# Attention of a hybrid block in half-height matmuls on eight cores: scores in three paired steps, values in two banks, filler in pairs of outputs

## The reference, cut to what matters

```python
q_nope, q_pe = q[..., :128], q[..., 128:]          # 128 + 64 dimensions
k_nope, v = kv[..., :128], kv[..., 128:]           # kv from the 512-wide latent c_kv
q_pe = apply_rope(q_pe, cos, sin); k_pe = apply_rope(k_rope, cos, sin)   # k_pe shared by all heads
sc = (q_nope . k_nope + q_pe . k_pe) * 192 ** -0.5   # key chunk <= query chunk, chunks of 64
out = softmax(sc) @ v;  y_attn = out * silu(z_attn)
```

## Time and profile before

| | |
|---|---|
| runs shown | 2835.36, 2835.76 (median), 3141.82 us |
| profiled execution | 2835.46 us |
| its span, slowest core (core 2) | 2832.8 us; all cores 2824.6 to 2832.8 us |
| granted TensorE clock, mean of cores | 0.994 to 0.997 of full speed |
| attention | from 1669 to 2376 us of the span |
| one head (heads 1 to 6, each) | 45.12 to 45.13 us |

### The profile page before, as it was taken

The page is one execution under the profiler, slowest core; times in us unless marked ns, Lnnn a source line. Parts: engine busy times, 40 slices in busy tenths (PEclk is TensorE's granted clock), DMA queues, the critical chain, the costliest instruction groups (busy, mean ns, idle before and its releaser), DMA issues.

```text
span 2832.8 us, 44730 instructions; the slowest of 8 cores (2824.6 to 2832.8 us)
## 1 busy us (share of the span) xinstructions
PE 2753.8 (97%) x16732; PEld 1563.5 (55%) x16732; DVE 985.0 (35%) x1675; ACT 819.0 (29%) x1365; POOL 376.5 (13%) x705
## 2 busy tenths in 40 slices
PE   6999999999999999999899999999999999999997
PEld 2455555555555554444799965555555554444443
DVE  3221112112211211111355546666666674121114
ACT  4210000000000001111476645656566563110013
POOL 0000000000000000000000014333333434000000
PEclk9999999999999999999999999999999999999998
DMA  9745555554545445554666420010100009954448
GB/s 262 142 74 79 83 79 81 80 83 79 80 79 82 79 80 81 94 99 77 186 191 205 147 42 16 16 23 16 24 16 16 16 1 198 232 87 78 80 83 283
DMA packets 94579, 265.66 MB, mean 94 GB/s; under 512 B 23968, under 2 KB 26144, under 8 KB 93344
## 3 DMA queue, kind: packets, MB, share of 16 engines
q0 software_dynamic: 39376, 148.91, 33.1%
q1 hardware_dynamic: 54992, 113.90, 13.2%
HBM read 390.71 MB, written 20.97 MB: 145 GB/s over the span
## 4 chain that ended last, share of the span: by engine, by line
PE 92%; DMA 3%; ACT 2%; issue 1%; POOL 1%; SPq 1%; DVE 1%; DVEq 0%; ACTq 0%; POOLq 0%
PE psall L290 92%; ACT arena L294 1%; DMA arena<-xo 1%; POOL arena L858 1%; DMA arena<-xres 1%; SPq L396 1%; DMA arena<-xt 1%; DVE arena L301 0%; DMA arena<-w_out_t 0%; SPq L392 0%; POOL arena L909 0%; DVEq L232 0%; ACT arena L297 0%; DVE arena L304 0%; ACTq L167 0%
## 5 line engine op out<-in xcount | busy, mean ns | idle before, releaser
L290 PE MATMUL psall<-arena 128*128 128x512 bf16 (+5 forms) x16732 | 2753.8, 327 | 59.1 <-ACT arena L294 22.6
L290 PEld LDWEIGHTS psall<-arena 128*128 128x128 bf16 x16732 | 1563.5, 98 | 1248.8 <-issue 96.7
L301 DVE TENSOR_TENSOR arena<-psall,arena 128x512 f32<-128x512 f32 (+3 forms) x378 | 225.6, 598 | 1252.9 <-PE psall L290 1230.2
L294 ACT ACTIVATE arena<-psall 128x512 bf16<-128x512 f32 (+7 forms) x706 | 447.5, 676 | 641.5 <-PE psall L290 426.3
L294 ACT ACTIVATE arena<-arena 128x768 bf16<-128x768 f32 (+7 forms) x487 | 313.0, 679 | 894.4 <-DVE arena L301 804.8
L301 DVE TENSOR_TENSOR arena<-arena 128x1024 f32<-128x1024 bf16 (+11 forms) x565 | 470.6, 847 | 194.4 <-ACT arena L294 117.5
L858 POOL TENSOR_SCALAR arena<-arena 128x64 bf16<-128x64 bf16 x512 | 258.4, 509 | 431.4 <-ACT arena L294 386.8
L363 POOL DMA_DIRECT2D arena<-w_in_t x95 | 67.1, 707 | 1292.5 <-PE psall L290 1195.7
L304 DVE TENSOR_SCALAR arena<-arena 128x192 bf16<-128x192 f32 (+3 forms) x440 | 137.7, 372 | 60.7 <-DMA arena<-xo 39.9
L297 ACT ACTIVATE arena<-arena 128x512 bf16<-128x512 f32 x64 | 40.3, 630 | 377.3 <-DVE arena L301 371.7
L307 DVE SCALAR_TENSOR_TENSOR arena<-arena 128x192 bf16<-128x192 f32 (+2 forms) x112 | 83.4, 750 | 76.0 <-ACT arena L294 69.3
(11 more groups left out here) (10 smaller groups left out, 9.4 us busy)
## 6 DMA issues: line engine op xcount, KB each, us to landing
arena<-w_in_t POOLq DMA_DIRECT2D x95, 1024.0 KB, 10.5
arena<-xt SPq DMA_DIRECT2D x128, 384.0 KB, 4.8
arena<-w_out_t POOLq DMA_DIRECT2D x64, 512.0 KB, 5.3
arena<-xo SPq DMA_DIRECT2D x32, 528.0 KB, 11.3
arena<-xres SPq DMA_DIRECT2D x6, 2048.0 KB, 47.3
out<-arena SPq DMA_DIRECT2D x8, 1536.0 KB, 12.5
arena<-w_uq_t POOLq DMA_DIRECT2D x16, 512.0 KB, 5.2
yc_spill<-arena SPq DMA_DIRECT2D x16, 256.0 KB, 8.1
```

The costliest lines, as they stand in the source:

```text
L290: P.add("pe", lambda e: e.matmul(out_, lhsT, rhs, start=start, stop=stop), reads=reads, writes=writes)
L294: P.add("act", lambda e: e.activation(out=out_, in_=in_, func=func, scale=scale, bias=bias), reads=reads, writes=writes)
L301: P.add(eng, lambda e: e.tensor_tensor(out=out_, in0=a, in1=b, op=op), reads=reads, writes=writes)
```

## The change

It touches attention and the first lines of the output projection.

1. Every matmul of attention uses 64 rows (partitions 0 to 63 or 64 to 127 of both operands; `LOHI`), issued in pairs, one of each row half, into two different banks. `mmr` records which row half last wrote a bank; when the other half writes it next, TensorE gets a wait on its own earlier matmul.
2. The rotary queries are folded: `q_out` writes the products to `TP`, a matmul with `dmat_bf` (ones at equal index modulo 64) sums the two parts, and `r_out` stores the result twice in `TQ`. Scores are then three pairs per unit instead of four matmuls: step 0 (tile 0 with rows 0 to 63, tile 1 with rows 64 to 127), step 1 (crosswise), step 2 (the rotary part, 64 rows for each tile).
3. Values: each key tile is two half matmuls, the lower rows into bank 4, the upper into bank 5, for either half of the queries. At the end of a half ScalarE copies bank 4 to `POS` and VectorE adds bank 5. `PV` of a half's first unit is held until the next unit.
4. The filler makes two outputs at a time, in banks 6 and 7, in two phases (each output gets one row half per phase), in chunks of four 512-column pairs. 26 chunks per head: 8 queries, 8 keys, 2 rotary sums, 8 values. A unit takes one chunk after `PV` and sometimes a second after `QK`; a chunk that starts a pair is only taken at the first place, where the sums of a half (`fin_b`) go too.
5. `fin_b` has four half matmuls in banks 6 and 7, a ScalarE copy, a VectorE addition, then Ln and Exp. There are two `ACC` instead of three.
6. The order of units is half 0 and then half 1, in each the widest and the narrowest in alternation (g = 0, 7, 1, 6, ... and 0, 15, 1, 14, ...). Within a unit `QK` step 0 comes first, then `PV` and filler, then steps 1 and 2.
7. In the output projection the first 16 matmuls per row tile go for tiles 0 to 3 first, then 4 and 5, and the weight loads of these come after them.

The diff, cut to its core:

```diff
-        seq = [(0, 0), (0, 1), (0, 2)]
-        for i in range(5):
-            seq += [(1, i), (0, 3 + i)]
-        seq += [(1, i) for i in range(5, 16)]
+        seq = []
+        for half, n in ((0, 8), (1, 16)):
+            for i in range(n // 2):
+                seq += [(half, i), (half, n - 1 - i)]
...
+        def mmr(r, bank, cs, lhsT, rhs, start, stop, reads):
+            ins = P.add("pe", lambda e: e.matmul(psb[bank][:, cs], lhsT, rhs, start=start, stop=stop), reads=reads, writes=[tps[bank]])
+            old = tile_of.get(bank)
+            if old is not None and old[0] != r:
+                old[1].signal = True
+                ins.deps.append(("c", old[1]))
+            tile_of[bank] = (r, ins)
...
+        def k_out(h, s, bank):
+            act(KH[h % 2][:, s * 512:(s + 1) * 512], psb[bank], AF.Copy, [tps[bank]], [t_kh[h % 2][s]])
...
+        def halves(banks, ops, phase, lo, hi):
+            for i in range(lo, hi):
+                for r in range(2):
+                    o = (r + phase) % 2
+                    cs, wf, xf, reads, st, sp = ops[o][i]
+                    mmr(r, banks[o], cs, wf(LOHI[r]), xf(LOHI[r]), i == 0 and phase == 0, sp and i == len(ops[o]) - 1 and phase == 1, reads)
+
+        def group(ops, n, fin):
+            out = []
+            for phase in range(2):
+                for lo in range(0, len(ops[0]), n):
+                    out.append([not out, lambda phase=phase, lo=lo: halves((6, 7), ops, phase, lo, min(lo + n, len(ops[0])))])
...
+            for r in range(2):
+                k2 = r if step == 0 else 1 - r
+                kt, bank, rows = 2 * g + k2, 2 * buf + k2, LOHI[r]
+                if step < 2:
+                    mmr(r, bank, slice(c0, 512), KH[hb][rows, kt * 128:(kt + 1) * 128], QN[hb][rows, half, c0:512], step == 0, False,
+                        [t_kh[hb][kt // 4], t_qn[hb][half]])
+                else:
+                    mmr(r, bank, slice(c0, 512), K2[rows, kt * 128:(kt + 1) * 128], TQ[hb][rows, half, c0:512], False, True,
+                        [t_k2[g], t_tq[hb][half]])
...
+                for r in range(2):
+                    mmr(r, 4 + r, slice(c0, 512), VH[vb][LOHI[r], kt, hp * 128:(hp + 1) * 128], PT[pb][LOHI[r], k2, c0:512], kt == 0,
+                        (half, g) in last_of and k2 == 1, [t_vh[vb][g], t_pt[pb]])
+            if (half, g) in last_of:
+                assert not open_pos
+                open_pos.append((h, half))
+                act(POS, psb[4], AF.Copy, [tps[4]], [t_pos])
+                tt(POS, psb[5], POS, ALU.add, [tps[5], t_pos], [t_pos])
...
+            act(rc[half], psb[banks[0]], AF.Copy, [tps[banks[0]]], [t_rc[half]])
+            tt(rc[half], psb[banks[1]], rc[half], ALU.add, [tps[banks[1]], t_rc[half]], [t_rc[half]])
+            act(rc[half], rc[half], AF.Ln, [t_rc[half]], [t_rc[half]])
...
+                def fill(pos):
+                    start = not fl or fl[0][0]
+                    if start and pend:
+                        hh, hf = pend.pop(0)
+                        fin_b(hh, hf, (6, 7))
+                        later(gi + 2, lambda: fin_c(hh, hf))
...
+                    if not fl or (pos == 2 and start):
+                        return 0
+                    if pos == 2 and (h == 15 or done >= nfl * (ui + 1) / 20):
+                        return 0
+                    fl.pop(0)[1]()
+                    return 1
...
                 if gi + 1 < ntot:
-                    QK(gi + 1)
+                    QK(gi + 1, 0)
                 soft(gi)
...
+                done += fill(1)
+                if gi + 1 < ntot:
+                    QK(gi + 1, 1)
+                    QK(gi + 1, 2)
+                done += fill(2)
```

More of the change, by code:

```diff
@@ L410, in build_program @@
         P.join(t_cst + [t_gin, t_ones, t_eps])
+        t_dbf = Tr("dbf")
+        P.add("dve", lambda e: e.tensor_copy(out=dmat_bf, in_=dmat), writes=[t_dbf])
         for b in range(NT0):
@@ L812, in filler, with qend @@
             if h + 1 < 16:
-                yield from fill_q(h + 1)
-                yield from fill_k(h + 1)
-            pr, hp = divmod(h, 2)
+                for bi in range(2):
+                    chunks += group((q_ops(h + 1, bi, 0), q_ops(h + 1, bi, 1)), 4,
+                                    lambda bi=bi: (q_out(h + 1, bi, 0, 6), q_out(h + 1, bi, 1, 7)))
+                last = chunks[-1][1]
+                def qend():
+                    last()
+                    if h + 3 < 16:
+                        hload(h + 3)
@@ new lines, in filler, with pbank @@
+            return chunks
+        pbanks = [6, 7, 0, 1, 2, 3]
+        npb = [0]
+        def pbank():
+            npb[0] += 1
+            return pbanks[npb[0] % 6]
+        for bi in range(2):
+            for part in range(2):
+                b = pbank()
+                whole(b, q_ops(0, bi, part))
+                q_out(0, bi, part, b)
+        hload(2)
+        for s in range(8):
+            b = pbank()
+            whole(b, k_ops(0, s))
+            k_out(0, s, b)
+            if s == 1:
+                for bi in range(2):
+                    b = pbank()
+                    whole(b, r_ops(bi))
+                    r_out(0, bi, b)
@@ L881, in fin_a, with fin_b @@
             act(HI[half], SA[half], AF.Copy, [t_sa[half]], [t_hi[half]])
             tt(LO[half], SA[half], HI[half], ALU.subtract, [t_sa[half], t_hi[half]], [t_lo[half]])
[L884 to L888, removed]
+        def fin_b(h, half, banks):
+            for src, tr, i in ((HI, t_hi, 0), (LO, t_lo, 1)):
+                for r in range(2):
+                    mmr(r, banks[r], slice(0, 512), ones_bf[LOHI[r], :], src[half][LOHI[r], :], i == 0, i == 1, [tr[half]])
+            act(rc[half], psb[banks[0]], AF.Copy, [tps[banks[0]]], [t_rc[half]])
+            tt(rc[half], psb[banks[1]], rc[half], ALU.add, [tps[banks[1]], t_rc[half]], [t_rc[half]])
+            act(rc[half], rc[half], AF.Ln, [t_rc[half]], [t_rc[half]])
@@ L971, in build_program @@
                     woload()
-        for gi in range(ntot, ntot + 7):
+        for gi in range(ntot, ntot + 4):
             if gi - 2 < ntot:
```

218 lines of the change are left out of this document (115 added, 103 removed).

## The result

The changed kernel is slower: 1.0622 times the time of the kernel before, 95% interval 1.0598 to 1.0646, about 3012 us against 2835.6. Its profiled execution took 3013.2 us, the span of the slowest core (core 4) is 3011.7 us.

The account below looks back on a forecast made before the run. TensorE's list was taken to bound the kernel. Per head, 40.7 us work, 9.1 bank waits and 4.0 score waits made 53.8 against 45.12; in all +128 on 2835.5 gave 2963 us, range 2865 to 3040.

Parts of the forecast that it names:

- A pair costs one slot: Attention matmuls: a pair of halves takes one 512-column full matmul's time, 0.216 us; a head's work is 40.7 us.
- a pair is not a pair: Rival on attention's half matmuls: halves run one after the other, 80.8 us a head, about 3385 us; chance 0.07.
- Waits for the filler banks: Banks 6 and 7, filled together: TensorE waits until both are emptied, 9.1 us a head.
- Waits for the scores: Score steps 1 and 2 behind the filler, bare last steps and ScalarE's in-order list: 4.0 us a head.
- the bare steps: Last four steps of a head mostly lack filler: 1.08 us of work against 1.44, 1.4 us for four.
- TensorE's waits on its own matmuls at nothing: Waits between row halves (`mmr`) cost nothing: `PV` and a chunk, 0.86 us and more, cover 0.16 + 0.14 us.
- The emptying of banks 4 and 5 at nothing: End of a values half: emptying takes 1.83 us, costed at nothing since the next half's first `PV` is held one step.
- The clock stays at full speed: TensorE's granted clock in attention heads stays at full speed, as before (1.00).
- Heads 14 and 15: Last two heads, with less filler: head 14 at 45.5 us, +8; head 15 at 35 us, -2 with 4 either way.
- The sum: Whole kernel: 14 x 8.7 = +122 us, head 14 +8, head 15 -2, preload +0.4; together +128 us.
- the waits don't show: Rival on attention: only TensorE's work counts, 42.2 us a head, 2790 us; chance 0.13.
- half of them: Rival on attention: half of the waits show, 5.5 us and 46.2 us a head, 2853 us; chance 0.09.

Follow-up runs that it names:

- e3: Changed kernel with only 64 of 512 columns of each filler output taken out of PSUM from head 2 on: 1.0337 times the kernel before.
- e11: Changed kernel with filler and sums as 128-row matmuls, one bank emptied while the other fills, sums without copy and addition: 1.0270 times the kernel before.
- e10: Changed kernel with the filler dealt out more slowly, at 26/22 instead of 26/20 chunks a step: 1.0528 times the kernel before.
- e2: Changed kernel with all three score steps issued before both filler places: 1.0580 times the kernel before.
- e7: Changed kernel with the matmuls of the sums (`fin_b`) put up two units later: 1.0703 times the kernel before.
- e8: Changed kernel with `fin_b` as two 128-row matmuls into one bank, without copy and addition: 1.0456 times the kernel before.
- e4: Kernel before with only the rotary queries folded and each unit's rotary scores as one pair of half matmuls: 1.0141 times the kernel before.

## Why the prediction was right

Sign and mechanism were as forecast; the time was 2963 us and is 3012, within the range, 72% of the move. By the prediction's steps:

- *A pair costs one slot*: right. 0.215 us against 0.216 of a full matmul; the head's list is 40.5 us against 40.7. Neither the 0.220 us that the prediction set beside it nor its 0.3 us for narrow pairs is seen: two pairs of 64 columns in a row start 0.028 to 0.033 us apart. The rival "a pair is not a pair" is out.
- *Waits for the filler banks*: right in kind, too small in size. 9.1 us forecast, 7.4 + 3.5 = 10.9 us in the trace. e3, which shortens the emptying alone, gives 5.8 us of it back; e11, which restores one bank after the other for filler and sums, gives 6.5 net of 5.4 for changeovers. The groups came out near the sum (7.4 against 7.0), `fin_b` not (3.5 against 2.1): the sum gave each wait the length of its own copies, and left out what stands before them in the list of their engine. The prediction named VectorE's additions as what would make it grow, but not the copy into `ACC` and `POS`.
- *Waits for the scores*: 4.0 forecast; 2.8 us by role in the changed kernel. Part of the 4.0, the bare steps, showed in e10 (1.6 us a head against 1.4). The reason given for the term, that steps 1 and 2 stand behind the filler, is not borne out: e2 takes them out from behind it, and step 0 still loses 3.3 us. What sets the rest of this wait stays open.
- *TensorE's waits on its own matmuls at nothing*: nearly right, 0.4 us at second phases.
- *The emptying of banks 4 and 5 at nothing*: wrong. The prediction asked only when the next `PV` could start. What it missed is who stands behind the addition in VectorE's list: the two outputs of a filler pair of queries, 0.6 us later for it. The timeline shows it; no run without the addition was made (e7 moved `fin_b` away, and the wait stayed; e11 kept the addition, and the wait went).
- *The clock stays at full speed*: wrong. After the wait of 2.3 us it fell in six of heads 1 to 13, about 1 us each, and the granted clock was 0.94 and 0.93 in heads 14 and 15.
- *Heads 14 and 15*: +8 and -2 forecast. From the start of the output projection, 2376.80 before and 2550.28 after, 173.5 us are lost ahead of it; 14 heads of 11.0 us make 154, the preload 0.4, so the last two cost 19. From first mask to first mask head 14 takes 53.4 us (forecast 45.5; 42.8 before), and head 15 takes 43.3 to the start of the projection (forecast 35; 33.1 before): both are 8 us over the forecast. In head 15, without filler, TensorE waits up to 2.8 us at a time for ScalarE and up to 1.8 for POOL: I had counted only the Exps.
- *The sum*: 14 x 8.7 = 122 was 154, the rest 6 was 20, and 5.4 us lie behind attention (456.0 and 461.4 us on the slowest cores). They are a difference between cores and not the change: core 2 takes 456.0 us there before and 455.9 after.

The rival "the waits don't show" gave 2790 us, and "half of them" 2853: both refuted. The Trainium skill (TensorEngine Tiling (Array Packing), section on the PSUM bottleneck) says that tiling speeds up TensorE but not the emptying of PSUM. The traces agree, in a form of their own: neither engine that empties is busy for more than 61% of a head (33.9 of 55.7 us). It is the moment that is bound, not the rate.

## What to carry to other kernels

Two outputs that are finished together need their banks emptied together, with nothing to cover it; before pairing outputs, compare the emptying of both (here 1.1 to 1.8 us) with the work that lies between two groups (0.77 us), and not the engines' busy shares. When an operation is added to the list of an in-order engine, list what stands behind it. Where half matmuls save a slot, count changeovers at 0.10 us each (48 of them cost more than 15 slots saved), and put the half ones together, away from short outputs.

## What the runs showed of the hardware

- Two 64-row matmuls of different row halves and banks take the time of one: pairs of 512 columns every 0.215 us, pairs of 64 columns every 0.028 us at best. Behind a full matmul the halves start 0.003 to 0.004 us apart (e4), in the changed kernel often 0.005 to 0.020.
- The two row halves need not keep step: in the changed kernel a 512-column half of filler starts at 1676.597 us, ahead of a 384-column half of the other row half, at 1676.630, that stands before it in the program.
- A changeover between 128-row and 64-row matmuls costs 0.10 us each way at 64, 192 and 512 columns (e4).
- TensorE's granted clock fell from 1.00 to 0.50 in attention after TensorE had stood for most of 2.3 us with one half matmul in between. The long wait alone doesn't settle it: it is at the start of each of heads 1 to 13, and the clock fell in six of them; in e10 it fell in all 13, and in e8, which has waits of up to 1.8 us at the same place, in none. What decides between them stays open.
